# Encoder layer on one core: keys and values stored in reverse token order, the bias table stored as one row per head, and the last product of the gate/up phase placed behind the first down granule

## The chip, the cores and the metric

One Trainium2 chip, one of its cores. The metric is the time of one execution on the device, in microseconds (us). The kernel before: median 1023.13 us of three runs (1022.89, 1023.13, 1027.93).

## What is computed

One layer of an encoder in float32, 512 tokens of width 1024:

```
x = x + 1/2 * SwiGLU_1(RMSNorm(x))          # d_ff 2816
h = RMSNorm(x)
[q | k | v | f | g_a | g_b] = h @ W_in
y_a = WindowAttention(q, k, v; sink, bias) @ W_a     # 8 heads of 64, 2 kv heads
y_b = Re(FFT2(f)) @ W_b
x = x + (sigmoid(g_a) * y_a + sigmoid(g_b) * y_b) @ W_out
x = x + 1/2 * SwiGLU_2(RMSNorm(x))
out = RMSNorm(x)
```

The attention works in blocks of 128 tokens; a query sees the keys at a distance of at most 128. The score of query i and key j gets a bias that depends on the head and on j - i alone: 257 values per head, taken from a table of 32 buckets. Distances beyond 128 are masked.

## The kernel before

Activations are kept transposed: feature on the partition, 512 tokens along the row. Every product is made in a split form: weight and activation are each a rounded part ("hi") and a rest ("lo"), and a product is hi times hi, hi times lo and lo times hi. So each weight tile that comes from memory (`raw`) is rounded by ScalarE into `w_hi` (L575), the rest is taken by VectorE into `w_lo` (L967, L1135), and then TensorE (PE) uses it. A *granule* is one such weight tile; four slots rotate. The semaphore `w_used` counts the granules that PE is done with, `w_hi_ready` and `w_lo_ready` those that are prepared.

A SwiGLU (r = 0 and r = 1) has a gate/up phase and a down phase. Of the 22 tiles of d_ff, the first 6 are made directly (L1582). The other 16 ("pairs", q = 0 to 15) are made from products of half matrices, 7 in place of 8 (Winograd's form). PE's order for a pair is in `pair_frame` (L1622): the groups G0, G1, G2 of the pair, each with two products of 12 matmuls 256 wide, and in between the product of G3 of the pair before, `last_product` (L1617). The latter adds to the right half of the bank z and may start when VectorE's `c2` (L1145) has read z (`z_read`). For the last pair, q = 15, it is issued in `ffn_down` (L1666), ahead of the down projection. Pair 0 has no `last_product` before it, so from its first product to the last of pair 15 there are 111.

The down phase makes 8 columns of 128 outputs, each from four granules of 6, 6, 6 and 4 tiles (`DOWN_TILES`). Its activations `a_t` must be rounded too, two tiles at a time, in the order `CONV`: ScalarE's `a_rounded` (L747) and VectorE's `a_rest` (L1184), together a *conversion*. Granule 0 needs the conversions 0 to 2, granule 1 the ones up to 5, granule 2 up to 8, granule 3 up to 10. Conversion 8 (tiles 12 and 13) writes over an operand of `last_product`. The conversions are interleaved with the end of the last pair by hand, in `last_pair` of ScalarE (L762) and of VectorE (L1190). There `c12` (L1154) adds up the right half of the gate, ScalarE's `silu_c12` follows, and `swiglu` (L1161) makes the tile.

SyncE issues the loads. `window_loads` (L466) brings a pair's four blocks of 256 KB. Those of pair 1 wait until VectorE has split granule 11, the last direct one. VectorE's `sums` (L1119) is the first to use a pair's blocks, then GpSimd (POOL) and ScalarE.

The bias: PE makes the 257 values per head, VectorE copies them into `bias_row` (8 heads on 8 partitions, masked values around), and ScalarE stores that row to memory 128 times per head (`bias_pieces`, L682: eight DMAs of 256 KB each, spread over `direct_pairs` of the first half). Much later (L851 to L854) one DMA reads it back with a row pitch that is one element shorter than the stored one, so that partition q gets its row shifted by q.

Keys (L1271) and values (L1280) are scaled by VectorE from PSUM into `ga_t` and `ua_t`, and then split or transposed. `window(nb)` (L145) names the key blocks of a query block and the first of the three blocks of bias to use. The order of all work in the mixer is a list written by hand, `MIXER` (L162).

## Time and profile before

| | |
|---|---|
| median of three runs | 1023.13 us |
| the profiled execution | 1025.82 us |
| its span | 1023.9 us |
| mean granted TensorE clock | 0.994 of full speed |
| PE matmul busy | 1002.1 us, 98% of the span |
| PE weight load busy | 890.4 us, 87% |
| VectorE (DVE) busy | 679.5 us, 66% |
| ScalarE (ACT) busy | 440.9 us, 43% |
| GpSimd (POOL) busy | 197.9 us, 19% |
| moved by DMA | 100.89 MB, mean 99 GB/s |
| of it, ScalarE's queue (q10) | 4.86 MB |
| pair block, 256 KB, to landing, median | 3.6 us |

Busy shares are averages over the whole span. With PE at 98%, time is lost or won only where PE waits or runs at the lower clock, so the views to read are PE's waits, and then the timelines around them. "Idle before" in brackets is the time for which the engine stood before the instruction, with what ended it. "SPq" and "ACTq" are the queues of DMA issues of SyncE and ScalarE; the length of a row there is that of issuing, not of the transfer. In a timeline, rows of matmuls overlap: their spacing is by their starts. Times in a timeline count from the start of the span.

### The profile page before, as it was taken

The page shows a single profiled execution, that of the slowest core. Times are in us where ns is not written, and L with a number is a line of the kernel's source. Part 1 is how long each engine was busy: PE and PEld are TensorE (multiplying, and loading weights), DVE is VectorE, ACT ScalarE, POOL GpSimd, SP SyncE. Part 2 cuts the span into 40 slices and gives each one's busy share as a digit, 9 for nine tenths or more (in the row PEclk, how much of TensorE's full clock was granted, in tenths as well). Part 3 has the DMA queues.
Part 4 walks back from the last instruction along what each step waited for, and adds up shares of the span by engine and source line. Part 5 has one row for each costly group of instructions (what it writes and reads, how often), then busy time and mean ns, then how long its engine had stood idle before and what let it go on. Part 6 is the DMA issues. An engine that isn't in the chain of part 4 may idle for free.

```text
span 1023.9 us, 16282 instructions
## 1 busy us (share of the span) xinstructions
PE 1002.1 (98%) x5872; PEld 890.4 (87%) x5872; DVE 679.5 (66%) x924; ACT 440.9 (43%) x656; POOL 197.9 (19%) x113
## 2 busy tenths in 40 slices
PE   8999999998999999999999999999999999899997
PEld 7788999998888888988888888888999999788887
DVE  5768998999444346767765555468898989933332
ACT  5334444546322234446664334334344444623322
POOL 2543343330011010000000002224243434001101
PEclk9999999999999999999999999999999999999999
DMA  6555333323323363312112343332242422333222
GB/s 208 131 106 134 100 106 110 95 82 102 99 86 100 108 186 84 106 39 65 54 51 83 98 126 103 103 93 72 83 123 82 123 83 81 103 98 98 87 67 83
DMA packets 192888, 100.89 MB, mean 99 GB/s; under 512 B 13440, under 2 KB 190672, under 8 KB 192720
## 3 DMA queue, kind: packets, MB, share of 16 engines
q1 hardware_dynamic: 190560, 95.50, 31.9%
q10 hardware_dynamic: 2288, 4.86, 2.5%
q8 instruction: 25, 0.41, 0.2%
q14 instruction: 15, 0.12, 0.0%
HBM read 96.15 MB, written 4.19 MB: 98 GB/s over the span
## 4 chain that ended last, share of the span: by engine, by line
PE 88%; DVE 3%; issue 2%; POOL 2%; DMA 1%; ACT 1%; SPq 1%; ACTq 0%; POOLq 0%; DVEq 0%
PE bank L1499 17%; PE bank L1500 17%; PE bank L1511 16%; PE bank L1608 10%; PE bank L1614 10%; PE bank L1610 10%; POOL ssum L1445 1%; SPq L475 1%; POOL t_sum L1458 1%; DVE t_lo L971 1%; DMA x_rows<-in_x_dram 1%; DMA raw<-in_w_up_dram 1%; PE bank L1776 1%; PE bank L1504 1%; PE bank L1477 1%
## 5 line engine op out<-in xcount | busy, mean ns | idle before, releaser
L575 ACT ACTIVATE w_hi<-raw 128x1024 fp32r<-128x1024 f32 (+2 forms) x202 | 181.9, 903 | 242.8 <-PE bank L1511 165.8
L967 DVE TENSOR_TENSOR w_lo<-raw,w_hi 128x1024 fp32r<-128x1024 f32 (+2 forms) x138 | 150.2, 1089 | 154.9 <-ACT w_hi L575 153.5
L1608 PE MATMUL bank<-t_hi,w_hi 128*128 128x256 f32 x896 | 227.1, 285 | 9.9 <-issue 8.0
L1610 PE MATMUL bank<-t_lo,w_hi 128*128 128x256 f32 x896 | 226.8, 285 | 0.0
L1608 PEld LDWEIGHTS bank<-t_hi,w_hi 128*128 128x128 f32 x896 | 173.6, 194 | 10.5 <-issue 8.4
L1610 PEld LDWEIGHTS bank<-t_lo,w_hi 128*128 128x128 f32 x896 | 173.7, 194 | 0.1
L1445 POOL TENSOR_TENSOR ssum<-ssum,sq 128x512 f32<-128x512 f32 x27 | 41.3, 1530 | 544.9 <-ACT sq L612 544.0
L1614 PE MATMUL bank<-t_hi,w_lo 128*128 128x256 f32 x896 | 145.5, 285 | 0.0
L1499 PE MATMUL bank<-a_hi,w_hi 128*128 128x512 f32 (+1 forms) x374 | 140.5, 380 | 0.0
L1500 PE MATMUL bank<-a_lo,w_hi 128*128 128x512 f32 (+1 forms) x374 | 139.5, 377 | 0.0
L1614 PEld LDWEIGHTS bank<-t_hi,w_lo 128*128 128x128 f32 x896 | 125.3, 194 | 0.0
L1135 DVE TENSOR_TENSOR w_lo<-raw,w_hi 128x1024 fp32r<-128x1024 f32 x64 | 91.4, 1427 | 7.8 <-ACT w_hi L575 7.8
L575 ACT ACTIVATE w_hi<-raw_b 128x1024 fp32r<-128x1024 f32 x64 | 60.7, 951 | 81.3 <-POOL raw_b L1465 43.7
L1135 DVE TENSOR_TENSOR w_lo<-raw_b,w_hi 128x1024 fp32r<-128x1024 f32 x64 | 92.8, 1450 | 3.6 <-ACT w_hi L575 3.5
L1511 PE MATMUL bank<-a_hi,w_lo 128*128 128x512 f32 (+1 forms) x374 | 91.1, 377 | 0.0
L1499 PE MATMUL bank<-h_hi,w_hi 128*128 128x512 f32 x208 | 81.9, 394 | 0.3 <-DVE ga_t L1285 0.3
L1499 PEld LDWEIGHTS bank<-a_hi,w_hi 128*128 128x128 f32 x374 | 70.8, 189 | 12.8
L1500 PEld LDWEIGHTS bank<-a_lo,w_hi 128*128 128x128 f32 x374 | 70.7, 189 | 12.7
L1500 PE MATMUL bank<-h_lo,w_hi 128*128 128x512 f32 x208 | 81.1, 390 | 0.0
L1511 PEld LDWEIGHTS bank<-a_hi,w_lo 128*128 128x128 f32 x374 | 67.8, 188 | 12.9
L1499 PE MATMUL bank<-hf_hi,w_hi 128*128 128x512 f32 x192 | 75.8, 395 | 0.0
L1500 PE MATMUL bank<-hf_lo,w_hi 128*128 128x512 f32 x192 | 75.1, 391 | 0.0
(230 smaller groups left out, 1496.9 us busy)
## 6 DMA issues: line engine op xcount, KB each, us to landing
raw<-in_w_down_dram SPq DMA_DIRECT2D x48, 384.0 KB, 3.0
raw_b<-in_w_up_dram SPq DMA_DIRECT2D x64, 256.0 KB, 3.6
raw<-in_w_up_dram SPq DMA_DIRECT2D x64, 256.0 KB, 3.6
raw<-in_w_up_dram SPq DMA_DIRECT2D x24, 512.0 KB, 3.9
raw<-in_w_in_dram SPq DMA_DIRECT2D x22, 512.0 KB, 3.7
raw<-in_w_down_dram SPq DMA_DIRECT2D x32, 128.0 KB, 2.2
raw<-in_w_out_dram SPq DMA_DIRECT2D x8, 512.0 KB, 3.4
x_rows<-in_x_dram SPq DMA_DIRECT2D x4, 512.0 KB, 7.6
```

The lines of the kernel that those rows point to most:

```text
L475: sp.dma_start(pair_raw[q % 2][:, pair_slot(r, group), at_:at_ + HK, :], w_up[r][:, row:row + HK, cols]).then_inc(pair_landed[q % 2], 16)
L575: return nc.scalar.activation(dst, src, ACT.Copy, scale=scale)
L967: vec.tensor_tensor(w_lo[:, s, 0:nk, :], raw[:, s, 0:nk, :], w_hi[:, s, 0:nk, :].bitcast(F32), ALU.subtract).then_inc(w_lo_ready, 1)
L971: return vec.tensor_tensor(dst, full, hi.bitcast(F32), ALU.subtract)
L1135: vec.tensor_tensor(w_lo[:, slot, 0:nk, :], pair_raw[q % 2][:, slot, 0:nk, :], w_hi[:, slot, 0:nk, :].bitcast(F32), ALU.subtract).then_inc ...
L1445: nc.gpsimd.tensor_tensor(ssum[:, :], ssum[:, :], sq[:, m % 2, :], ALU.add).then_inc(sum_added, 1)
L1499: nc.tensor.matmul(out_ap, w_hi[:, s, k, :], xh, start=first and i == 0, stop=False)
L1500: mm = nc.tensor.matmul(out_ap, w_hi[:, s, k, :], xl, start=False, stop=False)
L1511: mm = nc.tensor.matmul(out_ap, w_lo[:, s, k, :], x_parts(k)[0], start=False, stop=last and i == len(tiles) - 1)
L1608: nc.tensor.matmul(out_ap, w_hi[:, slot, at_ + k, :], hi[:, k, :], start=first and k == 0, stop=False, skip_group_check=not first)
L1610: nc.tensor.matmul(out_ap, w_hi[:, slot, at_ + k, :], lo_[:, k, :], start=False, stop=False, skip_group_check=not first)
L1614: mm = nc.tensor.matmul(out_ap, w_lo[:, slot, at_ + k, :], hi[:, k, :], start=False, stop=k == HK - 1, skip_group_check=not first)
```

## The change

`bias_row` is stored once, 16 KB, and the read takes for partition q the row from element q on: a step of +1 per partition where it was -1. So that this fits, the 257 values are written in reverse (`onehot`), and keys and values are written in reverse token order (a step of -1 in the two VectorE writes); `window` counts the blocks from the other end. And at the end of each gate/up phase PE does down granule 0 first, then `last_product` of pair 15, then granule 1. VectorE's `c2` is moved ahead by two conversions and a split, `c12` and `swiglu` by one conversion each; ScalarE's `silu_c12` comes one conversion earlier. Conversion 8 and the split of granule 3 wait for the count of `w_used` that `last_product` now has.

```diff
--- before.py
+++ after.py
@@ -138,14 +138,14 @@
     turn = 2 * np.pi * ((c[:, None] * c[None, :]) % FG_DIM) / FG_DIM
     tables = np.concatenate([pos, np.cos(turn), np.sin(turn)], axis=1).astype(np.float32)
     onehot = np.zeros((N_BUCKETS, NREL + 1), np.float32)
-    onehot[t5_buckets(), np.arange(NREL)] = 1.0
+    onehot[t5_buckets(), NREL - 1 - np.arange(NREL)] = 1.0
     return {"tables": tables, "onehot": onehot}
 
 
 def window(nb):
 
-    blocks = [j for j in (nb - 1, nb, nb + 1) if 0 <= j < TB]
-    return blocks, blocks[0] - (nb - 1)
+    blocks = [TB - 1 - j for j in (nb + 1, nb, nb - 1) if 0 <= j < TB]
+    return blocks, blocks[0] - (TB - 2 - nb)
 
 
 
@@ -230,7 +230,7 @@
     w_a = io["w_branch_a"][0]
     w_b = io["w_branch_b"][0].rearrange("(k p) n -> p k n", p=P)
     w_out = io["w_out"][0].rearrange("(k p) n -> p k n", p=P)
-    bias_rows = nc.dram_tensor("bias_rows", [N_HEADS, P, SEQ], F32, kind="Internal").ap()
+    bias_rows = nc.dram_tensor("bias_rows", [N_HEADS, SEQ], F32, kind="Internal").ap()
     steps = mixer_schedule()
 
     with ExitStack() as ctx:
@@ -653,39 +653,26 @@
                 silu(r, 1)
                 direct_hi(r, 7)
                 if r == 0:
-                    bias_pieces(0, 2)
+                    act.wait_ge(row_ready, 1)
+                    act.dma_start(bias_rows, bias_row[:, :]).then_inc(bias_stored, 16)
                 t_rounded(r, T_B11)
                 direct_hi(r, 8)
                 t_rounded(r, T_1)
-                if r == 0:
-                    bias_pieces(2, 2)
                 t_rounded(r, T_B21)
                 direct_hi(r, 9)
                 t_rounded(r, T_2)
                 silu(r, 2)
-                if r == 0:
-                    bias_pieces(4, 2)
                 t_rounded(r, T_4)
                 direct_hi(r, 10)
                 t_rounded(r, T_3)
                 t_rounded(r, T_B22)
                 silu(r, 3)
                 direct_hi(r, 11)
-                if r == 0:
-                    bias_pieces(6, 2)
                 group_hi(r, 0, G0)
                 silu(r, 4)
                 group_hi(r, 0, G1)
                 group_hi(r, 0, G2)
                 silu(r, 5)
-
-            def bias_pieces(piece, count):
-
-                act.wait_ge(row_ready, 1)
-                for i in range(piece, piece + count):
-                    act.dma_start(bias_rows[:, i * (P // 8):(i + 1) * (P // 8), :],
-                                  bias_row[:, :].unsqueeze(1).broadcast_to([N_HEADS, P // 8, SEQ])
-                                  ).then_inc(bias_stored, 16)
 
             def t_rounded(r, t):
 
@@ -750,7 +737,7 @@
                 if c < 6:
                     act.wait_ge(w_used, G_WIN[r] + window_count(PAIRS - 1, [G0, G0, G1, G1, G2, G2][c]) + 1)
                 elif c == 6:
-                    act.wait_ge(w_used, G_WIN[r] + window_count(PAIRS - 1, G3) + 1)
+                    act.wait_ge(w_used, G_DOWN[r] + 1)
                 else:
                     act.wait_ge(w_lo_ready, G_WIN[r] + window_count(PAIRS - 2, G3) + 1)
                 if 2 * c + 1 >= DIRECT:
@@ -773,13 +760,13 @@
                 a_rounded(r, CONV[3])
                 silu_c11(r, q)
                 split_hi(g + 1)
-                a_rounded(r, CONV[4])
-                a_rounded(r, CONV[5])
-                a_rounded(r, CONV[6])
+                for i in (4, 5, 6):
+                    a_rounded(r, CONV[i])
                 split_hi(g + 2)
-                for i in (7, 8):
-                    a_rounded(r, CONV[i])
+                a_rounded(r, CONV[7])
                 silu_c12(r, q)
+                a_rounded(r, CONV[8])
+                act.wait_ge(w_used, g + 1)
                 split_hi(g + 3)
                 for i in (9, 10):
                     a_rounded(r, CONV[i])
@@ -848,9 +835,8 @@
                         last.then_inc(proj_hi_ready, 1)
 
                         act.wait_ge(tab_lo_ready, 1)
-                        act.wait_ge(bias_stored, 16 * N_HEADS)
-                        diagonals = bias_rows.rearrange("h q m -> h (q m)")[:, BLK - 1:BLK - 1 + P * (SEQ - 1)]
-                        diagonals = diagonals.rearrange("h (q m) -> q h m", m=SEQ - 1)[:, :, 0:3 * BLK]
+                        act.wait_ge(bias_stored, 16)
+                        diagonals = bass.AP(bias_rows.tensor, 0, [[1, P], [SEQ, N_HEADS], [1, 3 * BLK]])
                         act.dma_start(bias[:, :, :], diagonals).then_inc(bias_landed, 16)
                     elif kind == "v":
                         split_hi(G_V + SLOTS)
@@ -1154,7 +1140,7 @@
             def c12(r, q, it=0):
 
                 dve.wait_ge(u2_ready, PAIRS * r + q + 1 + 2 * it)
-                dve.wait_ge(w_used, G_WIN[r] + window_count(q, G3) + 1 + 2 * SLOTS * it)
+                dve.wait_ge(w_used, G_WIN[r] + window_count(q, G3) + 1 + (q == PAIRS - 1) + 2 * SLOTS * it)
                 vec.tensor_tensor(gate_t[q % 2][:, HALF:SEQ], banks[z_bank(r, q % 2)][:, HALF:SEQ], u2_t[:, q % 2, :],
                                   ALU.add).then_inc(c12_ready, 1)
 
@@ -1200,17 +1186,16 @@
                 swiglu(r, q - 1)
                 split_lo(g)
                 a_rest(r, 2)
+                c2(r, q)
                 a_rest(r, 3)
                 split_lo(g + 1)
-                a_rest(r, 4)
-                c2(r, q)
-                a_rest(r, 5)
-                a_rest(r, 6)
+                for i in (4, 5, 6):
+                    a_rest(r, i)
                 split_lo(g + 2)
+                c12(r, q)
                 a_rest(r, 7)
-                c12(r, q)
+                swiglu(r, q)
                 a_rest(r, 8)
-                swiglu(r, q)
                 split_lo(g + 3)
                 a_rest(r, 9)
                 a_rest(r, 10)
@@ -1268,7 +1253,7 @@
                     elif kind == "k":
                         split_lo(G_K + SLOTS)
                         dve.wait_ge(w_used, G_K + 1)
-                        vec.tensor_tensor(ga_t[:, :], banks[O_K % BANKS][:, :], rstd[:, :], ALU.mult).then_inc(out_read, 1)
+                        vec.tensor_tensor(ga_t[:, ::-1], banks[O_K % BANKS][:, :], rstd[:, :], ALU.mult).then_inc(out_read, 1)
                         dve.wait_ge(proj_hi_ready, N_FGROUPS + 1)
                         for v in range(N_KV):
                             for to in range(2):
@@ -1277,7 +1262,7 @@
                     elif kind == "v":
                         split_lo(G_V + SLOTS)
                         dve.wait_ge(w_used, G_V + 1)
-                        vec.tensor_tensor(ua_t[:, :], banks[O_V % BANKS][:, :], rstd[:, :], ALU.mult).then_inc(out_read, 1)
+                        vec.tensor_tensor(ua_t[:, ::-1], banks[O_V % BANKS][:, :], rstd[:, :], ALU.mult).then_inc(out_read, 1)
                     elif kind == "q":
                         c = step[1]
                         dve.wait_ge(w_used, G_Q + c + 1)
@@ -1662,13 +1647,13 @@
                     o = O_DOWN[r] + c
                     pe.wait_ge(out_read, o - 1 + 2 * it)
                     if first:
-                        if c == 0:
-                            last_product(r, PAIRS - 1)
                         pe.wait_ge(c12_ready, PAIRS * (r + 1) - 1 + c)
                     for j in range(SLOTS):
                         g = G_DOWN[r] + SLOTS * c + j
 
                         if first and c == 0:
+                            if j == 1:
+                                last_product(r, PAIRS - 1)
                             need = len(CONV) * r + 1 + max(CONV.index(i // 2) for i in DOWN_TILES[j])
                             pe.wait_ge(a_hi_ready, need)
                             pe.wait_ge(a_lo_ready, need)
```

## Rows read from the trace of the kernel before

**Rows 1.** PE's waits over the whole span: waited for, us in total, times, longest us

```profile
PE bank L1608 <- issue: 8.0, 2, 4.1
...
PE bank L1608 <- DVE u_t L1142: 1.8, 1, 1.8
...
PE bank L1793 <- DVE pt_lo L971: 0.6, 1, 0.6
```

**Rows 2.** PE timeline, first half, end of gate/up: start us, us, engine line, instruction

```profile
245.82 0.64 PE L1614 MATMUL bank<-t_hi,w_lo 128*128 128x256 f32 x4
...
253.05 0.57 PE L1499 MATMUL bank<-a_hi,w_hi 128*128 128x512 f32 x1
...
257.33 0.39 PE L1499 MATMUL bank<-a_hi,w_hi 128*128 128x512 f32 x1
...
265.49 0.39 PE L1499 MATMUL bank<-a_hi,w_hi 128*128 128x512 f32 x1
...
268.21 0.39 PE L1499 MATMUL bank<-a_hi,w_hi 128*128 128x512 f32 x1
```

**Rows 3.** PE timeline, second half, the same place

```profile
883.50 0.64 PE L1614 MATMUL bank<-t_hi,w_lo 128*128 128x256 f32 x4
...
906.30 0.39 PE L1499 MATMUL bank<-a_hi,w_hi 128*128 128x512 f32 x1
```

**Rows 4.** VectorE timeline, first half, end of gate/up

```profile
244.83 2.36 DVE L971 TENSOR_TENSOR a_lo<-a_t,a_hi 128x1024 fp32r<-128x1024 f32 x2
...
247.10 0.95 DVE L967 TENSOR_TENSOR w_lo<-raw,w_hi 128x768 fp32r<-128x768 f32 x1
...
247.97 1.22 DVE L971 TENSOR_TENSOR a_lo<-a_t,a_hi 128x1024 fp32r<-128x1024 f32 x1
...
249.10 0.42 DVE L1148 TENSOR_TENSOR u_t<-bank,p_t 128x256 f32<-128x256 f32 x1
...
250.17 2.35 DVE L971 TENSOR_TENSOR a_lo<-a_t,a_hi 128x1024 fp32r<-128x1024 f32 x2
...
254.43 0.42 DVE L1158 TENSOR_TENSOR gb_t<-bank,u_t 128x256 f32<-128x256 f32 x1
```

**Rows 5.** PE timeline around pair 0 (both halves), and the clock in one window

```profile
83.84 0.64 PE L1614 MATMUL bank<-t_hi,w_lo 128*128 128x256 f32 x4
...
92.08 0.39 PE L1608 MATMUL bank<-t_hi,w_hi 128*128 128x256 f32 x1 [1.84 <-DVE u_t L1142]
...
725.10 0.64 PE L1614 MATMUL bank<-t_hi,w_lo 128*128 128x256 f32 x4
...
core 0: us, PE busy (x) PEld busy (x) DVE busy (x) ACT busy (x) POOL busy (x), PEclk, DMA share, GB/s
93.00:94.00 1.00, 1.00 (x7) 1.00 (x6) 1.00 (x2) 0.99 (x2) 0.00 (x0) 0.50 0.00 0
```

**Rows 6.** VectorE and SyncE's queue at pair 1's loads; SyncE's also in the second half

```profile
88.72 0.69 DVE L1125 TENSOR_TENSOR raw<-raw 128x512 f32<-128x512 f32 x1 [3.54 <-DMA raw<-in_w_up_dram]
...
71.11 13.40 SPq L475 DMA_DIRECT2D raw<-in_w_up_dram  x4
...
711.52 2.02 SPq L475 DMA_DIRECT2D raw<-in_w_up_dram  x4
```

**Rows 7.** Issues of the stores over the span; ScalarE's queue and loads, 60 to 80 us

```profile
L686 ACTq DMA_DIRECT2D bias_rows<-bias_row x8: 271/334/4572, 42.0 to 64.6; - x8
...
q10 hardware_dynamic: 525, 1.01, 42.6%
...
raw<-in_w_up_dram SPq DMA_DIRECT2D x3, 256.0 KB, 10.3
```

**Rows 8.** The bias read (KB, us to landing); writes of the Fourier branch, forwards and backwards

```profile
bias<-bias_rows ACTq DMA_DIRECT2D x1, 1536.0 KB, 8.9
...
L1308 DVE TENSOR_TENSOR y_t<-even_t,bank x4: 415/421/424, 413.8 to 442.4; 128x257 f32<-128x257 f32 x4
...
L1310 DVE TENSOR_TENSOR y_t<-even_t,bank x4: 415/415/417, 414.1 to 442.8; 128x255 f32<-128x255 f32 x4
```

**Rows 9.** ScalarE timeline, first half: conversion 8

```profile
253.29 1.06 ACT L575 ACTIVATE a_hi<-a_t 128x1024 fp32r<-128x1024 f32 x1 [2.40 <-PE bank L1614]
```

## The prediction

> **What bounds the kernel now.** I read first who waits for whom on TensorE, over the whole span. TensorE (PE) is the bound: it hardly waits, and the waits it has are few and large. Two pauses of about 4 us are put down to "issue" in front of L1608, and one of 1.8 us is put down to VectorE's L1142 [rows 1]. Every microsecond taken from these three comes off the span, since nothing else decides; the others beyond the start-up are below 1 us each, like L1793's 0.6 [rows 1].
>
> The timeline of PE shows where the two large ones lie: at the end of each gate/up phase. The last full product starts its last four matmuls at 245.82 and the first down granule begins at 253.05 [rows 2]; in the second half the same pair is 883.50, with column 1 starting at 906.30 [rows 3]. Between the last full product and the down projection stands `last_product` of pair 15 (L1666), which waits for `z_read`, the VectorE step `c2`. VectorE's timeline has that step at 249.10, behind two conversions, a split and a third conversion [rows 4]: its operand was there at 246.46, and PE stood for it.
>
> The third pause is in pair 0 of the first half. PE starts the last four matmuls of the first product at 83.84 in the first half and 725.10 in the second, and of the last of 111 products at 245.82 and 883.50. So 110 products took 161.98 us against 158.40 us (1.44 each) with the same code [rows 2, 3, 5]: the first half lost 3.58 us. PE stood from 90.08 to 92.08 (the trace counts 1.84 us of it as idle), and after that the granted clock was 0.50 of full speed, 1.2 instead of 2.4 GHz [rows 5]: the clock is the other 1.6 us of the loss.
>
> **Where the 3.58 us come from.** VectorE stood 3.54 us for the loads of pair 1 (88.72, L1125 [rows 6]), then came L1126, `up`, `swish` and `u2`, for which PE waited until 92.08. SyncE needed 13.40 us to issue these four loads; in the second half 2.02 us for the same four [rows 6]. What differs between the halves in that stretch is ScalarE's eight stores to `bias_rows`, 256 KB each, issued at 42.0 to 64.6 us, the slowest taking 4.57 us to issue; from 60 to 80 us they alone took 42.6% of sixteen engines' time, and loads needed 10.3 us to land [rows 7]; 3.6 is their median over the span.
>
> **The change, part by part.**
>
> *Bias stored once (L686, L851 to L854).* Eight stores, 2 MB, become one of 16 KB (8 rows of 2 KB). ScalarE's queue loses seven issues. If the loads of pair 1 land before VectorE is free for them (88.72 less 3.54: 85.18 [rows 6]), the chain from L1125 to PE's restart, 92.08 - 88.72 = 3.36 us, ends at 88.54, before PE gets to the product that needs it at 90.08 [rows 5]. The pause goes, and with it the slow clock: gain 3.6 us. Bounds: nothing, if the loads stay late for another reason; not more than 3.6, since the second half, with no stores, shows what is left. I take 3.6, because the second half is the same code. Before 82.9 us PE has work without a gap, so faster ScalarE issues buy nothing there.
>
> *Diagonal read.* Still one transfer of 1536 KB to 128 partitions in rows of 1536 bytes; only its source shrinks to 16 KB. It took 8.9 us from 406.7 us [rows 8], and the first score needs it at about 450.6, so it has 35 us of cover. I take 0; below nothing no gain can show, as PE does not wait for it; above, see the slower rival.
>
> *Keys and values mirrored.* Two VectorE writes with a negative step, 512 wide. The kernel has one already: L1310 writes 255 elements backwards in 415 ns, L1308 writes 257 forwards in 421 ns [rows 8]. I take 0. If a mirrored write took twice its 0.68 us, PE, which does not pause between 395 and 445 us, hides it. The window function yields as many blocks as before for each query block, and score, transpose and value matmuls keep shape and number: 0.
>
> *The last product behind down granule 0, first half.* PE's next product would start at 246.30 (245.82 + 0.48). Granule 0 (tiles 14 to 19) needs only conversions 0 to 2. Number 2 is the first of the two VectorE instructions at 244.83, done at 246.05 [rows 4]: no wait. A six-tile granule is 4.08 us (257.33 to 265.49 is two) and the four-tile one 2.72 (265.49 to 268.21) [rows 2]. Granule 0 ends at 250.38. `c2` now follows conversion 2: it starts at 246.50, when PE is done with the bank, takes 1.07 (249.10 to 250.17), and the product is not kept waiting: 250.38 to 251.82.
>
> Then VectorE is the question. Steps by the spacing of their starts [rows 4]: a conversion 1.135 (244.83 to 247.10 for two), a split of six tiles 0.87 (247.10 to 247.97), `c12` 0.34 (its 0.42 at 254.43 less the overlap of 0.08), `swiglu` 0.60, like the second half of `c2`. From 247.57: conversion 3, split 1, conversions 4, 5. Conversion 5 starts at 250.71 and ends at 251.93. Granule 1 needs it: it starts at 251.97, a wait of 0.15. Then conversion 6, split 2 (to 253.85), `c12`, conversion 7 (to 255.32), `swiglu` (255.92), conversion 8, which ends at 257.14. Granule 2 (tiles 8 to 13) needs conversion 8 and would start at 251.97 + 4.08 = 256.05; it waits until 257.18, so 1.13 us. **This is a new wait**: conversion 8 overlies the operand of the last product (L753) and stood free before. ScalarE is not the one who decides: its part of conversion 8, which in the kernel before came 2.40 us after the work ahead of it, for the product [rows 9], now comes right after the silu at 254.30 and ends at 255.66. Granule 3's split waits for one more count (w_used g+1), long there. Queued behind it are conversions 9 and 10, done on VectorE at 260.0; granule 3 starts at 261.26. SyncE's loads for column 1 wait for these splits: the latest comes 1.2 us later than before (258.3 for 257.1), and its granule is 18 us away.
>
> Column 1 starts at 257.18 + 4.08 + 2.72 = 263.98 instead of 268.21: gain 4.2.
>
> *Second half.* Same steps, from 883.98 on PE and 884.18 for `c2` (883.50 + 0.64 + 0.04): conversion 8 ends 10.64 later, at 894.82, column 1 starts at 901.66 instead of 906.30 [rows 3]: gain 4.6.
>
> **Bounds of these two.** If both new waits vanish, 1.3 more on each side. The unknown price is the clock after a pause of 1.13 us: after 0.6 us (L1793) the rows show no fall, after 1.84 us they show the lower level and a loss of 1.6 [rows 1, 5]. 1.13 is nearer to 0.6, so I take none; the other end is 1.6 on each side.
>
> The Trainium skill ("TensorE: Matmul & The Clock Gate", Part 1) says that what the clock looks at runs freely and does not start with the kernel, so the point of a change differs from run to run. By that rule the same pause may cost nothing in one run and the 1.6 in the next; no row here repeats a pause of that length.
>
> **Sum.** 3.6 + 4.2 + 4.6 = 12.4 us. The profiled execution took 1025.82 us (span 1023.9 and 1.9 around it): 1013.4. It is 2.7 us above the median of the other three runs (1022.89, 1023.13, 1027.93). If part of that 2.7 is how hard the stores hit the loads in a run, it goes with the stores and 1013.4 stands; if it is something else, it is 1010.7. A value between, nearer to the former: **1012.5**.
>
> **The rivals.**
>
> *The clock falls after the new wait, on both sides.* Placed at the start of granule 2, 257 and 895 us; 1013.4 + 3.2 = 1016.6, or 1014 against the median. For: the trace has a pause of 1.84 us that did it. Against: 0.6 did not. Chance 0.22.
>
> *The first pause stays.* SyncE's long issues would then come from its own loads. Gain 8.8: 1017.0. Against: the second half. By a rule of the Trainium skill ("DMA: Bandwidth & Descriptors", Queues, rings and completion order) an engine takes turns between the queues at packet granularity; two queues would then share evenly. Taken alone that doubles a load's 3.6 us to 7.2, and pair 1's loads, issued from 71.1 on, would have landed near 80, before VectorE wants them, so the stores would be no full explanation; the trace shows 10.3 us to landing [rows 7], more than the rule gives. Chance 0.10.
>
> *The wait only moves.* VectorE is full from 246.5 to 260 on; if its steps are 10% slower beside PE's reads, conversion 8 is late by 1 us more on each side, the clock falls too: 1013.4 + 2 + 3.2 = 1018.6. Chance 0.08.
>
> *Slower: the diagonal read from eight hot rows.* 128 partitions read the same 16 KB. It decides from the point where the read takes more than 44 us (five times 8.9). The stores moved 1.01 MB in 20 us, 50 GB/s [rows 7]; at half of that 1.57 MB take 63 us, the first score waits from 450.6 until 470, 19 us: 1013.4 + 19 = 1032, slower. For: nothing in the trace reads so small a source so often. Against: its rows are no smaller and no more than before. Chance 0.03.
>
> *The forecast* has 0.57, its own range 1010 to 1015.
>
> **How the numbers follow.** About 0.5% (5 us) is what a measurement of this kernel tells from no change. Forecast, clock and remaining pause (0.57 + 0.22 + 0.10) end below 1018: 0.89, less 0.02 for things unseen, 0.87. Within 0.5%: 0.10. Slower: 0.03. The range from 1009.5 (both new waits shorter, against the median) to 1017.5 (the pause stays) leaves out most of the moved wait, the slow read and what is unseen.
>
> **What would show it.** In the changed profile: no entry for L1142 in PE's waits and the granted clock 1.00 from 90 to 100 us; four L475 issues of pair 1 within 3 us; 110 products of the first half in 158.4 us; no "issue" of 4 us before L1608; instead a wait of about 0.15 us before granule 1 and 1.1 us before granule 2, released by VectorE's L971; column 1 about 17.7 us after the last full product. Wrong it would be if PE waited at 450 us for the bias, if a 3.6 us loss stayed in the first half, or if granule 2 waited for more than 2 us.

## The result and the profile after

| | before | after |
|---|---|---|
| device time, median | 1023.01 us (4 runs, 1022.60 to 1027.93) | 1013.60 us (4 runs, 1010.35 to 1014.11) |
| profiled execution (span) | 1025.82 (1023.9) | 1014.11 (1012.3) |
| bytes and packets on ScalarE's queue (q10) | 4.86 MB, 2288 | 2.78 MB, 1216 |

The ratio is 0.989 with an interval of 0.9854 to 0.9927; the changed kernel, run again in five rounds, gave 1012.68 us (1012.18 to 1012.90) against 1023.75, 0.989 again [0.9873, 0.9907]. It is faster by 1.1%, and 1012.5 had been forecast. Lines of the changed kernel are shifted: L1608, L1610 and L1614 are L1593, L1595 and L1599, L1499 is L1484, VectorE's L971 is L957, L1148 is L1134.

PE's waits over the whole span, the largest five (columns as in [rows 1]):

```profile
PE bank L1536 <- DMA x_rows<-in_x_dram: 3.2, 1, 3.2
PE bank L1484 <- ACT a_hi L575: 1.7, 2, 0.9
PE bank L1543 <- POOL half L1421: 1.7, 1, 1.7
PE bank L1834 <- ACT sq L931: 0.7, 1, 0.7
PE bank L1778 <- DVE pt_lo L957: 0.6, 1, 0.6
```

Both entries of [rows 1] that the prediction was about, three pauses in all, are gone: no "issue", no L1142 (now L1128). In their place stands one new entry, twice 0.9 us, in front of L1484, a down granule. Where it lies shows in PE's timeline, first half then second; the rows answer to [rows 2, 3]:

```profile
84.45 0.64 PE L1599 MATMUL bank<-t_hi,w_lo 128*128 128x256 f32 x4
...
242.85 0.64 PE L1599 MATMUL bank<-t_hi,w_lo 128*128 128x256 f32 x4
243.33 0.47 PE L1484 MATMUL bank<-a_hi,w_hi 128*128 128x512 f32 x1
...
247.54 0.28 PE L1593 MATMUL bank<-t_hi,w_hi 128*128 128x256 f32 x1
...
249.05 0.47 PE L1484 MATMUL bank<-a_hi,w_hi 128*128 128x512 f32 x1
...
254.26 0.47 PE L1484 MATMUL bank<-a_hi,w_hi 128*128 128x512 f32 x1 [0.86 <-ACT a_hi L575]
...
261.15 0.39 PE L1484 MATMUL bank<-a_hi,w_hi 128*128 128x512 f32 x1
...
876.35 0.64 PE L1599 MATMUL bank<-t_hi,w_lo 128*128 128x256 f32 x4
...
887.76 0.47 PE L1484 MATMUL bank<-a_hi,w_hi 128*128 128x512 f32 x1 [0.88 <-ACT a_hi L575]
...
894.68 0.39 PE L1484 MATMUL bank<-a_hi,w_hi 128*128 128x512 f32 x1
```

Read them as distances. From pair 0's first product (84.45) to the last full product (242.85) are 158.40 us for 110 products; it was 161.98. Granule 0 begins 0.48 us after the start of that product's last four matmuls, the last product follows at 247.54, granule 1 at 249.05, granule 2 after a wait at 254.26, column 1 at 261.15: 18.30 us, where it was 22.39. In the second half it is 18.33 us, where it was 22.80.

The granted clock stays at its upper level (2.4 GHz) behind the wait. Windows, with the PEclk column third from the end, as in [rows 5]:

```profile
92.00:94.00 2.00, 2.00 (x19) 2.00 (x18) 1.63 (x3) 1.29 (x2) 0.00 (x0) 1.00 0.31 88
254.00:256.00 2.00, 1.74 (x8) 1.49 (x9) 2.00 (x4) 2.00 (x4) 0.00 (x0) 1.00 0.01 3
256.00:258.00 2.00, 2.00 (x11) 1.65 (x10) 2.00 (x3) 0.58 (x1) 0.00 (x0) 1.00 0.44 129
```

VectorE's timeline over the same stretch (to be laid beside [rows 4]):

```profile
243.53 0.42 DVE L1134 TENSOR_TENSOR u_t<-bank,p_t 128x256 f32<-128x256 f32 x1 [0.46 <-PE bank L1599]
...
246.60 3.49 DVE L957 TENSOR_TENSOR a_lo<-a_t,a_hi 128x1024 fp32r<-128x1024 f32 x3
...
252.34 0.68 DVE L1152 TENSOR_TENSOR a_t<-gb_t,ub_t 128x512 f32<-128x512 f32 x1
252.94 1.22 DVE L957 TENSOR_TENSOR a_lo<-a_t,a_hi 128x1024 fp32r<-128x1024 f32 x1
```

The row of three conversions is numbers 4 to 6. Conversion 8 (252.94) ends at 254.16, and PE's granule 2 starts at 254.26. The wait is put down to ScalarE's half of that conversion, which had been done earlier: the step that came last is VectorE's, and the order of the starts tells it where the releaser's name does not. 254.16 is 10.63 us after `c2`'s start; by the prediction's steps it was 10.64.

At the other end, pair 1's loads on SyncE's queue; the loads from 60 to 80 us (KB each, us to landing); and the VectorE row that had stood 3.54 us for them [rows 6]:

```profile
71.71 2.02 SPq L475 DMA_DIRECT2D raw<-in_w_up_dram  x4
```
```profile
raw<-in_w_up_dram SPq DMA_DIRECT2D x4, 256.0 KB, 3.8
```
```profile
82.61 0.69 DVE L1111 TENSOR_TENSOR raw<-raw 128x512 f32<-128x512 f32 x1
```

2.02 us for four issues instead of 13.40, 3.8 us to landing instead of 10.3, and no idle time in front of the sum. The bias read lands in 6.7 us instead of 8.9 (other profiles of either form come closer to each other, see the rivals below), and the write of the mirrored keys takes 684 ns, within the 0.68 us that the prediction had for the plain one:

```profile
bias<-bias_rows ACTq DMA_DIRECT2D x1, 1536.0 KB, 6.7
```
```profile
L1256 DVE TENSOR_TENSOR ga_t<-bank,rstd x1: 684/684/684, 398.9 to 398.9; 128x512 f32<-128x512 f32 x1
```

The span fell by 11.6 us. The three stretches give 3.58 + 4.09 + 4.47 = 12.1, the rest between them 0.1. The start-up gave 0.6 back: pair 0's first product comes at 84.45 us for 83.84, PE having waited 3.2 us for `x_rows` instead of 2.2. The removed stores lie in that stretch (42.0 to 64.6 us), but its scatter does not follow them: it ends at 81.84 to 83.84 us in the five profiles with stores from 8 partitions and at 80.56 to 84.45 us in the nine without. So below a second measure stands beside the time: **the rest**, from the start of those four matmuls of pair 0's first product to the end of the span. It is 1023.9 - 83.84 = 940.06 us before and 927.85 after (927.90 in the repeat), 12.2 us apart, with the start-up's scatter taken out.

### The profile page after: what moved, and what is told of

The parts are those of the page before. It is cut to its first block and busy times, and to the rows that moved or that the text cites. A ratio compares the mean times of both kernels' runs of the same rounds, so it can differ in the third digit from the quotient of the medians.

```text
span 1012.3 us, 16276 instructions
## 1 busy us (share of the span) xinstructions
PE 997.7 (99%) x5872; PEld 885.7 (87%) x5872; DVE 679.0 (67%) x924; ACT 440.1 (43%) x656; POOL 198.1 (20%) x113
## 3 DMA queue, kind: packets, MB, share of 16 engines
q10 hardware_dynamic: 1216, 2.78, 0.8%
HBM read 96.15 MB, written 2.11 MB: 97 GB/s over the span
## 5 line engine op out<-in xcount | busy, mean ns | idle before, releaser
L1595 PE MATMUL bank<-t_lo,w_hi 128*128 128x256 f32 x896 | 224.7, 283 | 0.0
L1593 PE MATMUL bank<-t_hi,w_hi 128*128 128x256 f32 x896 | 224.6, 283 | 0.0
L1595 PEld LDWEIGHTS bank<-t_lo,w_hi 128*128 128x128 f32 x896 | 172.0, 192 | 0.2
L1593 PEld LDWEIGHTS bank<-t_hi,w_hi 128*128 128x128 f32 x896 | 172.0, 192 | 0.2
L1599 PE MATMUL bank<-t_hi,w_lo 128*128 128x256 f32 x896 | 144.0, 283 | 0.0
L1484 PE MATMUL bank<-a_hi,w_hi 128*128 128x512 f32 (+1 forms) x374 | 140.6, 380 | 1.7 <-ACT a_hi L575 1.7
L1599 PEld LDWEIGHTS bank<-t_hi,w_lo 128*128 128x128 f32 x896 | 123.6, 192 | 0.0
L1484 PEld LDWEIGHTS bank<-a_hi,w_hi 128*128 128x128 f32 x374 | 70.3, 188 | 15.4 <-ACT a_hi L575 2.5
L1484 PE MATMUL bank<-h_hi,w_hi 128*128 128x512 f32 x208 | 81.9, 394 | 0.3 <-DVE ga_t L1270 0.3
L1484 PE MATMUL bank<-hf_hi,w_hi 128*128 128x512 f32 x192 | 76.2, 397 | 0.0
```

The costliest lines, as they stand in the source:

```text
L1484: nc.tensor.matmul(out_ap, w_hi[:, s, k, :], xh, start=first and i == 0, stop=False)
L1593: nc.tensor.matmul(out_ap, w_hi[:, slot, at_ + k, :], hi[:, k, :], start=first and k == 0, stop=False, skip_group_check=not first)
L1595: nc.tensor.matmul(out_ap, w_hi[:, slot, at_ + k, :], lo_[:, k, :], start=False, stop=False, skip_group_check=not first)
L1599: mm = nc.tensor.matmul(out_ap, w_lo[:, slot, at_ + k, :], hi[:, k, :], start=False, stop=k == HK - 1, skip_group_check=not first)
```

## The experiments

**1. The two halves of the change, each alone.** One kernel took only the edits of the bias and the token order (`bias_rows` as one row per head, the diagonal read, the mirrored writes, the window function):

```diff
-                    bias_pieces(0, 2)
+                    act.dma_start(bias_rows, bias_row[:, :]).then_inc(bias_stored, 16)
...
-                        vec.tensor_tensor(ga_t[:, :], banks[O_K % BANKS][:, :], rstd[:, :], ALU.mult).then_inc(out_read, 1)
+                        vec.tensor_tensor(ga_t[:, ::-1], banks[O_K % BANKS][:, :], rstd[:, :], ALU.mult).then_inc(out_read, 1)
```

> The kernel before with the bias part alone (stored once, table, keys and values reversed); the order at the end of gate/up as before. My theory: the 110 products of the first half take 158.4 us instead of 162.0, the two pauses of 4 us at the ends of gate/up stay, and the time is 3.6 us below the kernel before (0.4%). Rival (the pause stays, SyncE's own loads are slow): 162.0 us and no change. Rival (the read of 16 KB is slow or the reversed writes cost): the first half gains, but PE waits near 450 us and the time is no better.

The other took only the new order at the end of gate/up, on ScalarE, VectorE and PE:

```diff
-                        if c == 0:
-                            last_product(r, PAIRS - 1)
...
+                            if j == 1:
+                                last_product(r, PAIRS - 1)
```

> The kernel before with the new order at the end of gate/up alone; eight stores as before. My theory: the first half still takes 162.0 us for its 110 products; from the last full product to column 1 it is 18.3 and 18.3 us instead of 22.4 and 22.8; the time is 8.6 us below the kernel before (0.8%). Rival (the two parts depend on each other): the sum of this gain and the one of the bias part alone misses the whole change's 11.6 us of span by more than 1 us.

Measured: 1021.40 us for the bias part, ratio 0.9974 [0.9964, 0.9985], and 1014.33 for the order, 0.9907 [0.9884, 0.993], against 1024.47. The waits and SyncE's queue of the first:

```profile
PE bank L1594 <- issue: 7.9, 2, 4.0
```
```profile
70.15 2.02 SPq L475 DMA_DIRECT2D raw<-in_w_up_dram  x4
```

The loads are quick again, the 110 products take 158.39 us, and the two long pauses at the ends stay. PE's timeline of the second shows the reverse, the pause at pair 0 still there:

```profile
89.71 0.39 PE L1607 MATMUL bank<-t_hi,w_hi 128*128 128x256 f32 x1 [1.39 <-DVE u_t L1142]
```

Its ends are 18.33 and 18.29 us. So the mechanisms sit where the prediction put them, but their sizes do not add up, and the second expectation named that as its rival: the rests are 936.14 and 929.96 us, gains of 3.92 and 10.10 on 940.06, together 14.0 for the 12.2 of both. On top of the other part each is worth less: the new order 8.3 us (936.14 to 927.85), the stores 2.1 us (929.96 to 927.85). With the pause in place this kernel's 110 products took 160.49 us, not 161.98, and the granted clock behind it was 1.00. The pause cost 2.1 us here. The 3.58 of the prediction held a fall of the clock that this run did not have.

**2. Are the stores the cause?** The changed kernel, with eight stores put back that nobody reads, in the old form (8 partitions, each row of 2 KB sent 16 times) and at the old places:

```diff
+                    act.dma_start(spare_rows[:, i * (P // 8):(i + 1) * (P // 8), :],
+                                  bias_row[:, :].unsqueeze(1).broadcast_to([N_HEADS, P // 8, SEQ])
+                                  ).then_inc(spare_stored, 16)
```

> The changed kernel plus eight stores of the same form and size as before (256 KB each, from the 8 partitions of the bias row) at the same places, to memory that nobody reads. The result does not depend on them. My theory (the stores are the cause, not the way the bias is read): the pause in front of pair 0's last product is back, the 110 products take about 162 us, SyncE's issues for pair 1 take over 10 us again. Rival (the cause was the ScalarE queue's eight issues or the layout of the read): the products stay at 158.4.

The same eight issues and the same 2 MB, but from a tile with 128 partitions, in rows of 512 bytes:

```diff
+                    act.dma_start(spare_rows[i, :, :, :], ones[:, :].unsqueeze(1).broadcast_to([P, 4, P])
+                                  ).then_inc(spare_stored, 16)
```

> The changed kernel plus eight stores of 256 KB each, at the same places, but from a tile of 128 partitions (512 bytes per row) to memory that nobody reads: the same bytes and the same number of issues, 16 DMA engines instead of 8. The result does not depend on them. Theory A (what hurts is that the stores come out of 8 partitions, slowly, and hold half of the engines until 87 us): they are gone soon after each issue, pair 1's loads are issued within 4 us, and the products take 158.4 us. Theory B (2 MB of extra traffic hurt however they are spread): the loads are late again and the products take 160 us or more.

Measured: 1015.59 and 1010.28 us, one run each. With the old form, SyncE's queue, the transfers from 60 to 80 us and PE at pair 1:

```profile
71.07 12.99 SPq L477 DMA_DIRECT2D raw<-in_w_up_dram  x4
```
```profile
q10 hardware_dynamic: 524, 1.01, 42.3%
...
raw<-in_w_up_dram SPq DMA_DIRECT2D x3, 256.0 KB, 10.3
```
```profile
91.67 0.39 PE L1610 MATMUL bank<-t_hi,w_hi 128*128 128x256 f32 x1 [1.49 <-DVE u_t L1145]
```

With the wide form:

```profile
67.88 2.02 SPq L477 DMA_DIRECT2D raw<-in_w_up_dram  x4
```
```profile
q10 hardware_dynamic: 1056, 0.52, 8.7%
...
raw<-in_w_up_dram SPq DMA_DIRECT2D x4, 256.0 KB, 3.5
```

The late loads and long issues of [rows 6, 7] come back with the stores, to the tenth of a microsecond in the landing time, and none of it with the same bytes from 128 partitions: 110 products in 160.51 us with the one, 158.40 with the other. It is neither the bytes nor ScalarE's issues but the shape: 1.01 MB held 42% of sixteen engines' time in the one form, 0.52 MB held 8.7% in the other, 2.5 times less per byte, and SyncE's issue of other loads stretched from 2.02 to 12.99 us. What the loads of pair 1 were spared is the stores' presence: the wide ones were through by 64 us, before these loads were issued (67.88), the narrow ones were under way until 85 us. So the run shows that wide stores are gone in time; what they do to a load beside them it does not show. The Trainium skill ("DMA: Bandwidth & Descriptors", Rules for kernel authors) says that an outermost dimension of less than 16 confines a transfer to at most that many engines; these stores have 8 there, the wide ones 128, and the two runs agree with it: from 80 to 83 us the narrow stores held 47 to 48% of sixteen engines' time, just under the half that eight can give, and the wide ones held 97% in their last microsecond (63 to 64 us). The row length changed along with the partitions (2 KB to 512 bytes), and no run separates the two.

**3. What of the new order does the work?** The prediction spoke of the last product "behind down granule 0", which is PE's order. In the changed kernel PE's order, and the counts of `w_used` that belong to it, were set back, and VectorE's and ScalarE's kept:

```diff
+                        if c == 0:
+                            last_product(r, PAIRS - 1)
...
-                            if j == 1:
-                                last_product(r, PAIRS - 1)
```

> The changed kernel with PE's order undone: the last product again ahead of granule 0 (and the counts that follow from it). VectorE and ScalarE keep the new order, so c2 stays early. Theory A (VectorE's order bounds the end of gate/up; PE's order matters little): PE waits 1.3 us for c2, then nothing before granule 2, and column 1 comes 18.3 us after the last full product, as in the changed kernel; time within 1 us of it. Theory B (the gain comes from granule 0 covering the wait): column 1 comes 1.3 us later or more on each side (the clock may fall), 3 us or more in all.

The changed kernel itself, unchanged, in the same rounds:

> The changed kernel once more, as the measure for the three that follow, on the same chip: about 1013 us; PE's two waits for conversion 8 of 0.9 us.

And the opposite: in the kernel before, one line of VectorE's program moved, nothing else, all eight stores kept:

```diff
                 a_rest(r, 2)
+                c2(r, q)
                 a_rest(r, 3)
                 split_lo(g + 1)
                 a_rest(r, 4)
-                c2(r, q)
```

> The kernel before with one line moved: VectorE's c2 of the last pair directly behind conversion 2. PE's order, ScalarE's order, all counts and the eight stores as before. Theory A (c2's place on VectorE is what the move of the change is worth): PE waits 1.3 us for c2 on both sides in place of 4, the clock stays at 1.00, column 1 comes 18.4 us after the last full product instead of 22.4 and 22.8, and the time is that of the move alone, 8 to 9 us below the kernel before. Theory B (granule 0 has to cover the wait): 20 us or more, half of the gain.

Measured: 1012.61 us (1012.12 to 1013.45; ratio 0.9891) with PE's order back, against 1012.68 for the changed kernel in the same five rounds: no difference. And 1015.78 us for the moved line, 0.9911 [0.9894, 0.9929] against 1025.40: this one line is worth 9.6 us (7.3 to 10.9 by the interval). PE's timeline of the two:

```profile
242.58 0.36 PE L1592 MATMUL bank<-t_hi,w_hi 128*128 128x256 f32 x1 [1.29 <-issue]
```
```profile
91.69 0.39 PE L1608 MATMUL bank<-t_hi,w_hi 128*128 128x256 f32 x1 [1.75 <-DVE u_t L1142]
...
246.24 0.35 PE L1608 MATMUL bank<-t_hi,w_hi 128*128 128x256 f32 x1 [1.29 <-issue]
```

(The first row is of the changed kernel with PE's order back, the other two of the moved line; the pause of 1.75 us is that of pair 0, whose stores are still there.) The profile names no releaser for the waits of 1.29 us, but the order of the times does: the first half of `c2` ends at 242.48 us in the first kernel, and PE starts at 242.58. With PE's old order it waits 1.29 us for `c2` and not for conversion 8; with the new order it does not wait for `c2` and stands 0.9 us for conversion 8. The ends are 18.42 us for 18.33. The wait of 1.29 us was not moved away by the headline edit; it was exchanged. What took the 4 us away was that `c2` no longer stands behind conversions 3 and 4 and a split: PE's last product starts 1.44 us late instead of 4.05, and the clock does not fall.

**4. The wait that is left.** In the changed kernel conversion 8 was put ahead of `swiglu` and of granule 2's split on VectorE (PE needs that split only for the granule's last six matmuls), and ahead of `silu_c12` on ScalarE. VectorE's part:

```diff
-                split_lo(g + 2)
                 c12(r, q)
                 a_rest(r, 7)
-                swiglu(r, q)
                 a_rest(r, 8)
+                swiglu(r, q)
+                split_lo(g + 2)
                 split_lo(g + 3)
```

> The changed kernel with conversion 8 ahead of the silu on ScalarE, and on VectorE c12, conversions 7 and 8 ahead of swiglu and of granule 2's split. My theory (granule 2 waits for VectorE's order, not for the last product as such): both waits of 0.9 us vanish, from the last full product to column 1 it is 17.4 us on both sides instead of 18.3, and the time is 1.8 us below the changed kernel. Rival (the wait only moves on): granule 2's split or conversion 10 is late by as much, and PE waits in front of granule 3.

1010.33 us (1009.65 to 1011.61), ratio 0.9864 [0.9846, 0.9882], in the same five rounds in which the changed kernel gave 1012.68 and no run of it was below 1012.18. PE's timeline:

```profile
242.45 0.64 PE L1599 MATMUL bank<-t_hi,w_lo 128*128 128x256 f32 x4
...
248.65 0.47 PE L1484 MATMUL bank<-a_hi,w_hi 128*128 128x512 f32 x1
...
252.82 0.39 PE L1484 MATMUL bank<-a_hi,w_hi 128*128 128x512 f32 x1
```

No wait before granule 2 (252.82), no entry for it in PE's waits, 17.2 us for either end, 1.1 less per side. **This is the best version found.** The same order on VectorE and ScalarE, with PE's order set back:

> The better order of VectorE and ScalarE (conversion 8 first) with PE's order undone. If PE's order is worth nothing only because VectorE is the bound behind it, its worth shows here: PE waits 1.3 us for c2 and column 1 comes 18.4 us after the last full product, 1.2 us later than with both on each side (17.2), in all 2.4 us of time. Rival (PE's order is worth nothing in any case): 17.2 us here too.

1012.70 us (1010.48 to 1013.83), and the wait of 1.29 us for `c2` is back on both sides, ends of 18.42 us. The rest is 928.14 us for 925.65. The medians of the two are from different rounds and the runs of the latter scatter by 3.4 us, so the profiles' stretches decide here. PE's order is worth 1.2 us per side, but only once conversion 8 is early too. The two edits pay together or not at all: each alone leaves PE to wait for the other thing.

**5. What does the length of a pause do to the clock?** VectorE was given idle copies ahead of `swiglu`, so that the wait before granule 2 grows:

```diff
+                vec.tensor_copy(y_t[:, :], rstd[:, :])
+                if r == 1:
+                    vec.tensor_copy(even_t[:, 0:HALF], rstd[:, 0:HALF])
                 swiglu(r, q)
```

> The changed kernel with extra VectorE copies of unused data ahead of swiglu in the last pair: 0.6 us in the first half, 1.0 us in the second, so that granule 2 waits 1.5 us in the first half and 1.9 us in the second. The result does not depend on them. Theory A (the clock falls after a pause somewhere between 0.9 and 1.84 us): in the second half the granted clock goes to 0.50 soon after and costs about 1.6 us more. Theory B (a fall depends on more than the length of the pause): 1.9 us leave the clock at 1.00, and column 1 moves by the copies' length alone.

The copies took half of what was assumed (0.34 and 0.20 us by the spacing of the starts), so the pauses came to 1.19 and 1.39 us, the clock stayed at 1.00, and the time was 1013.59 us. That tests little, and the next one was made with products of two tiles, whose duration the trace had shown (0.60 and 0.34 us):

```diff
+                vec.tensor_tensor(y_t[:, :], rstd[:, :], rstd[:, :], ALU.mult)
+                vec.tensor_tensor(even_t[:, 0:HALF], rstd[:, 0:HALF], rstd[:, 0:HALF], ALU.mult)
+                if r == 1:
+                    vec.tensor_tensor(sq[:, 1, HALF:SEQ], rstd[:, 0:HALF], rstd[:, 0:HALF], ALU.mult)
                 swiglu(r, q)
```

> The changed kernel with extra VectorE work on unused data ahead of swiglu in the last pair: 0.93 us in the first half, 1.26 us in the second, so that PE stands 1.8 us and 2.1 us before granule 2. The result does not depend on it. Theory A (a pause of 1.8 us or more brings the lower clock, as the one of 1.84 did): the granted clock is 0.50 behind both or behind the longer, and granule 2 takes up to 1.6 us longer. Theory B (it is not the pause's length alone): clock 1.00 behind both, granule 2 takes 4.1 us.

And the kernel before once more, unchanged:

> The kernel before, unchanged, for a second profile. The three runs with the stores on paused 1.39, 1.49 and 1.75 us in front of pair 0's last product and kept the clock, where the first profile paused 1.84 and lost it. If length decides, this run pauses 1.4 to 1.8 with the clock at 1.00 (110 products in 160.5 to 160.8 us) or over 1.8 with the clock at 0.50 (162 us). If it is chance, a pause of 1.8 or less can come with the lower clock, or a longer one without. The two pauses of 4 us at the ends of gate/up should bring the lower clock as in the other two profiles that had them.

The first gave 1015.66 us. Its pauses in PE's timeline, and the windows in and behind them:

```profile
254.42 0.47 PE L1488 MATMUL bank<-a_hi,w_hi 128*128 128x512 f32 x1 [1.82 <-ACT a_hi L575]
...
889.21 0.47 PE L1488 MATMUL bank<-a_hi,w_hi 128*128 128x512 f32 x1 [2.14 <-ACT a_hi L575]
```
```profile
256.00:258.00 2.00, 2.00 (x11) 1.63 (x10) 2.00 (x4) 0.00 (x0) 0.00 (x0) 1.00 0.45 131
...
890.00:892.00 2.00, 2.00 (x10) 1.66 (x9) 2.00 (x3) 0.00 (x0) 0.00 (x0) 1.00 0.37 106
```

Pauses of 1.82 and 2.14 us, as long as the one of 1.84 behind which the clock was halved in [rows 5], and none of it here. The kernel before, run again (1025.45 us, span 1023.7), shows the same for its own pause at pair 0, and the opposite for its long ones:

```profile
91.14 0.39 PE L1608 MATMUL bank<-t_hi,w_hi 128*128 128x256 f32 x1 [1.22 <-DVE u_t L1142]
...
248.28 0.55 PE L1608 MATMUL bank<-t_hi,w_hi 128*128 128x256 f32 x1 [3.89 <-issue]
```
```profile
247.00:248.00 1.00, 0.00 (x0) 0.00 (x0) 0.97 (x3) 1.00 (x3) 0.00 (x0) 0.52 0.48 140
...
250.00:252.00 2.00, 2.00 (x9) 1.81 (x9) 2.00 (x3) 0.78 (x1) 0.00 (x0) 0.50 0.00 0
```

From 247 to 248 us the clock is already low, while PE still stands. In the first profile of this kernel the low stretch begins at 250.0, also ahead of PE's start at 250.35:

```profile
250.00:251.00 1.00, 0.65 (x3) 0.68 (x4) 1.00 (x2) 0.88 (x1) 0.00 (x0) 0.50 0.82 245
```

That stretch ended at about 253.4 us. Here the low clock lasted until about 253.9, though PE had restarted 2.07 us earlier than there (248.28 for 250.35): more of PE's work met the slow clock, and the end is the longer one, 23.60 us for 22.39.

The 110 products took 160.23 us in this profile, 161.98 in the first; the ends 23.60 and 23.42 us, 22.39 and 22.80 in the first. The rest is 940.2 us for 940.1. Two profiles of one kernel agree in the total and differ by 1.8 us at one place and by 1.2 and 0.6 at two others.

## Why the prediction was right

The stretches of the profiles, in us (the ends run from the last full product's last four matmuls to column 1):

```
kernel                       110 products   end 1    end 2
before                          161.98      22.39    22.80
before, second profile          160.23      23.60    23.42
one line moved (c2)             160.77      18.42    18.42
new order alone                 160.49      18.33    18.29
stores put back                 160.51      18.31    18.31
changed                         158.40      18.30    18.33
changed, PE's order back        158.40      18.42    18.42
changed, conversion 8 first     158.40      17.20    17.21
```

**The sum.** 3.6 + 4.2 + 4.6 = 12.4 was forecast against the profiled execution, and 12.2 came out of these three stretches and what lies between them. The start-up took 0.6 back, and 1014.11 stands against the 1013.4 of the sum; against medians 1012.5 meets 1013.60 and 1012.68. That each term fits so closely is in part luck: they were taken from the one profile that they are compared with. Against the second profile of before the three stretches give 1.8, 5.3 and 5.1 us, again 12.2 in all.

**The stores.** The chain from SyncE's long issues over the late loads to PE's pause was right, and experiment 2 shows it. The size of the term is what was off. The prediction took 3.58 us, "because the second half is the same code". That is what one profile lost. The profiles of four kernels with these stores (second profile of before, order alone, one line moved, stores put back) lost 1.8, 2.1, 2.4 and 2.1, with pauses of 1.2 to 1.75 us and no fall of the clock. Nor need the clock be all of the 1.6 us that the prediction put down to it: with the stores put back and the clock at 1.00, PE restarts 1.64 us late and loses 2.11, the other half microsecond in slower starts behind the pause and in a second short stop at 96.4 us. The bias part alone gained 3.1 us between medians (1024.47 less 1021.40), 1.5 to 3.7 by its interval, which holds either size; its profile's rest is 3.9 below 940.06, but a single profile of before can carry the fall or not.

**The ends.** 4.2 and 4.6 were forecast, 4.09 and 4.47 measured, and the steps of VectorE's schedule held to 0.1 us over ten of them. Two things in the working were looser than the result. First, it named the gain after PE's new order ("The last product behind down granule 0"), as if granule 0 covered the wait. Experiment 3 shows that the order of VectorE alone brings it; the prediction's own steps held this, since they priced `c2` at 246.50 only because it no longer follows the conversions. Second, the term was one difference of two rows (22.39 less 18.16) and so held the clock's part unseen. With PE's order set back, an end is 18.42 us, of which 1.44 are that the last product starts at 242.58 instead of 0.48 behind 240.66; without a wait it is 16.98. In the kernel before that product starts 4.05 us late in both profiles (250.35 and 248.28), so 1.4 of the 22.39 and 2.6 of the 23.60 are slow clock. A fall of the clock in or right behind each of the long pauses was thus paid for in both profiles of the kernel before, and went with them.

**The new waits.** The one before granule 2 was forecast at 1.13 us, for conversion 8. Its row says 0.86, but counts only from the modelled end of the last pipelined matmul; by the starts, granule 2 would follow granule 1 (249.05) after 4.08 us, at 253.13, and starts at 254.26, 1.13 late. The end with conversion 8 first is shorter by as much, 17.20 for 18.30. The wait of 0.15 before granule 1 has no idle row; by the starts (248.49 and 0.48, for 249.05) it is 0.08. Two of the prediction's signs were off: it announced column 1 "about 17.7 us" after the last full product where its own steps give 18.16 (263.98 less 245.82) and 18.30 was measured, and it expected the wait to be put down to VectorE's L971, where the profile names ScalarE.

**The rivals.** The clock after the new wait (0.22) did not fall, here or in any profile with that wait. The first pause (0.10) did not stay: experiment 2 shows that the stores are the whole of it. The 7.2 us that the prediction worked out from taking turns between two queues fell short of the 10.3 measured, in the run with the stores put back as well. But equal turns are equal bytes only if the packets are alike, and in the profile with the stores put back those of the stores averaged 1.9 KB (1.01 MB in 524) and those of the loads 0.5 KB (0.63 MB in 1270, 60 to 80 us). So the shortfall says nothing against turns; no run tests them. The wait did not move (0.08): VectorE's steps beside PE were not slower. The diagonal read from few rows (0.03) was not slow: it landed in 6.3 to 7.7 us in the ten profiles that have it, the old one in 7.3 to 8.9 in four, and PE never waited for it near 450 us.

**Left open.** Of the pauses of 1.19 to 2.14 us behind the start-up, fourteen in eight profiles kept the clock and one (1.84 us, [rows 5]) did not. Length alone does not decide. Nor does the fall wait for PE's restart: of the six pauses of 3.9 to 4.2 us, all with a fall, in four the low clock begins 0.4 to 2.0 us ahead of it, in two it begins with the restart or 0.2 us behind; the fall behind the pause of 1.84 us came 0.9 us after it. The Trainium skill ("TensorE: Matmul & The Clock Gate", Part 1) says that what the clock looks at runs freely, so that the same work can meet it at another phase in each run; the runs agree with that, but none of them shows the phase. What makes the start-up scatter by 4 us was not tried: the waits for `x_rows` differ (1.5 to 3.2 us), and the clock in the first 84 us.

## What to carry to other kernels

When a wait is in front of an engine, look first at the order of the engine that makes it wait: one line of VectorE's program gave 9.6 us, and reordering the bound engine, PE, gave nothing until the next late step had been moved too. Follow a removed wait to the step that is late next, and price both together. A term taken from one profile's stretch should be split into idle time and clock before it is used, since the clock's part differs between runs. And a transfer's cost to others is in its shape: with 2 MB of stores from 8 partitions another queue's loads landed in 10.3 us, with the same bytes from 128 partitions, in shorter rows, in 3.5, because these stores were done before the loads began.

## What the runs showed of the hardware that was not expected

- Issuing four loads took SyncE 12.84 to 13.40 us beside the 8-partition stores of another engine's queue (five profiles), and 2.02 us without them, as with 128-partition stores of the same bytes, which were through by 64 us.
- 1536 KB read from a source of 16 KB, in overlapping rows by all 128 partitions, landed in 6.3 to 7.7 us (ten profiles), no slower than from a source of 2 MB (7.3 to 8.9, four profiles).
- A VectorE copy of 128x512 in fp32 spaces the next start by 0.34 us, a product of two such tiles by 0.60.
- In or within 0.2 us behind every pause of about 4 us of PE the granted clock fell to 0.50, in all three profiles that had them (before twice, bias part alone), in four of the six before PE started again; pauses of 1.82 and 2.14 us left it at 1.00.
